# First MLP of a two-layer model: the v half before the u half, with LayerNorm and token mixing inside the groups of u

## The reference, cut to what matters

```python
def gmlp_mixer(h, w_in, b_in, ln_g, ln_b, w_s, b_s, w_out):
    B, S, _ = h.shape
    z = jax.nn.gelu(h @ w_in + b_in)
    u, v = jnp.split(z, 2, axis=-1)
    v = layer_norm(v, ln_g, ln_b)
    v = v.reshape(B, S // CHUNK, CHUNK, GMLP_GROUPS, GMLP_GROUP_DIM)
    causal = jnp.tril(jnp.ones((CHUNK, CHUNK), dtype=w_s.dtype))
    ws = w_s * causal[None]
    v = jnp.einsum('gts,bnsgc->bntgc', ws, v) + b_s.T[:, :, None]
    y = u * v.reshape(B, S, GMLP_WIDTH)
    return y @ w_out
```

## Time and profile before

| what | value |
|---|---|
| median of 3 runs | 2139.59 us (2136.43 to 2139.62) |
| the profiled execution, its own time | 2142.33 us |
| its span in the trace | 2140.6 us |
| mean granted TensorE clock | 0.971 of full speed |
| PE, share of the span | 93% |
| DVE, ACT, POOL | 39%, 33%, 48% |
| PE's share of the chain that ended last | 84% |
| first matmul of u, of v, of mlp_out | 52.9, 151.1, 264.3 us |

### The profile page before, as it was taken

One profiled execution on the slowest core, in us unless ns is written; L12 is line 12 of the kernel. 1 busy time (PEld: TensorE's weight loads), 2 busy tenths in 40 slices (PEclk: granted clock), 3 DMA queues, 4 the chain that ended last, 5 costly groups with the idle time before them and its releaser, 6 DMA issues.

```text
span 2140.6 us, 28567 instructions
## 1 busy us (share of the span) xinstructions
PE 1993.2 (93%) x10804; PEld 1703.4 (80%) x10804; DVE 836.9 (39%) x1442; ACT 714.4 (33%) x1112; POOL 1029.4 (48%) x553
## 2 busy tenths in 40 slices
PE   5999898999999979998998999999889998978997
PEld 5889887888888868876877888888767997856997
DVE  5545656534443066252635111100537730036212
ACT  3422334222221244444634222212433223335323
POOL 1644374466664435546634655544333343605552
PEclk9999999899999999999999999999999999998999
DMA  7645334465656213222112333322212325201132
GB/s 255 220 168 172 113 109 132 138 190 170 196 167 206 90 49 91 78 85 88 44 39 60 103 94 97 98 94 93 72 59 70 99 89 91 89 20 40 60 99 79
DMA packets 220321, 230.62 MB, mean 108 GB/s; under 512 B 15456, under 2 KB 185224, under 8 KB 219960
## 3 DMA queue, kind: packets, MB, share of 16 engines
q1 hardware_dynamic: 219712, 229.01, 34.8%
q10 hardware_dynamic: 504, 0.15, 0.0%
HBM read 226.33 MB, written 2.79 MB: 107 GB/s over the span
## 4 chain that ended last, share of the span: by engine, by line
PE 84%; DVE 6%; ACT 4%; issue 2%; POOL 1%; DMA 1%; ACTq 1%; DVEq 1%; SPq 0%; POOLq 0%
PE acc L1344 66%; PE aux L1344 4%; PE ms L625 3%; PE acc L600 2%; PE ms L1344 2%; PE ada_ps L1344 1%; PE aux L614 1%; PE ada_ps L1505 1%; DVE tmp L1946 1%; DMA x_tok<-in_x 1%; PE aux L1595 1%; PE aux L1632 1%; POOL w_lo L736 1%; DVE score L2160 1%; DVE ada_acc L1842 0%
## 5 line engine op out<-in xcount | busy, mean ns | idle before, releaser
L736 POOL TENSOR_TENSOR w_lo<-raw,w_hi 128x1024 fp32r<-128x1024 f32 (+1 forms) x296 | 742.4, 2522 | 639.8 <-ACT w_hi L729 639.4
L1344 PE MATMUL acc<-hh,w_hi 128*128 128x512 f32 (+1 forms) x1472 | 562.7, 382 | 45.8 <-issue 21.5
L1344 PE MATMUL acc<-hh,w_lo 128*128 128x512 f32 (+1 forms) x1472 | 555.1, 377 | 0.0
L1344 PE MATMUL acc<-hl,w_hi 128*128 128x512 f32 (+1 forms) x1472 | 554.9, 377 | 0.0
L729 ACT ACTIVATE w_hi<-raw 128x1024 fp32r<-128x1024 f32 (+1 forms) x296 | 308.4, 1051 | 409.6 <-DMA raw<-in_ffn_w_down 152.8
L1344 PEld LDWEIGHTS acc<-hh,w_hi 128*128 128x128 f32 x1472 | 285.2, 194 | 104.4 <-issue 48.6
L1344 PEld LDWEIGHTS acc<-hl,w_hi 128*128 128x128 f32 x1472 | 285.6, 194 | 49.3 <-issue 1.7
L1344 PEld LDWEIGHTS acc<-hh,w_lo 128*128 128x128 f32 x1472 | 285.0, 194 | 49.1
L1344 PE MATMUL acc<-w_hi,hh 128*128 128x256 f32 x704 | 201.1, 286 | 0.0
L1344 PE MATMUL acc<-w_hi,hl 128*128 128x256 f32 x704 | 199.2, 283 | 0.0
L1344 PE MATMUL acc<-w_lo,hh 128*128 128x256 f32 x704 | 199.2, 283 | 0.0
(11 more groups left out here) (472 smaller groups left out, 2972.8 us busy)
## 6 DMA issues: line engine op xcount, KB each, us to landing
raw<-in_ffn_w_gu SPq DMA_DIRECT2D x176, 256.0 KB, 3.2
ada_raw<-in_ada_w SPq DMA_DIRECT2D x80, 512.0 KB, 3.9
raw<-in_w_in SPq DMA_DIRECT2D x52, 512.0 KB, 3.4
raw<-in_ffn_w_down SPq DMA_DIRECT2D x44, 512.0 KB, 3.6
raw<-in_a_w_in SPq DMA_DIRECT2D x32, 512.0 KB, 4.8
raw<-in_a_w_out SPq DMA_DIRECT2D x16, 512.0 KB, 3.8
ada_raw<-in_kv_ada_w SPq DMA_DIRECT2D x16, 512.0 KB, 4.8
raw<-in_kv_w SPq DMA_DIRECT2D x16, 512.0 KB, 3.7
```

The source lines that it names most:

```text
L736: eng.tensor_tensor(w_lo[:, s, part, :], raw[:, s, part, :], w_hi[:, s, part, :].bitcast(F32), ALU.subtract).then_inc(w_split, 1)
L1344: ins = pe.matmul(out, w, x, start=first and n == 0, stop=last and n == len(pairs) - 1, skip_group_check=check)
```

## The change

v goes first, u second. The sixteen transposes go into group 1 of v, the row sums into groups 3 and 5, the spreading of the gain into group 7, each ahead of chunk 4 and with more PSUM banks. u follows; from its group 1 on, two mixings are put ahead of chunks 2 and 5 of each group. The last two mixings go ahead of chunks 2 and 3 of `mlp_out`. DVE handles a pair of mixings at the start of its work for a u group and the modulation slot after it. On ACT and POOL the rounding of a pair is part of the epilogue of a u group; the last pair and all weight units of `mlp_out` from unit 2 on come after it, in that order. In SP's list the slots 16 to 19 go behind units 2, 4, 6 of the first half and unit 0 of the second, and `ws_raw` is loaded into another place, two waits later. The first unit of `mlp_out` is computed with `apart`.

```diff
-            load_stage(sp, "mlp_u", lambda i, j: ada_slot_load(sp, 2 * i + j), skip=2, unroll=True)
-            load_stage(sp, "mlp_v", lambda i, j: ada_slot_load(sp, 8 + 2 * i + j), unroll=True)
+            load_stage(sp, "mlp_v", lambda i, j: ada_slot_load(sp, 2 * i + j), skip=2, unroll=True)
+            load_stage(sp, "mlp_u", lambda i, j: ada_slot_load(sp, 8 + 2 * i + j), unroll=True)
...
-            load_out("mlp_out", {(0, 7): 16, (1, 2): 17, (1, 3): 18, (1, 4): 19})
+            load_out("mlp_out", {(0, 2): 16, (0, 4): 17, (0, 6): 18, (1, 0): 19})
...
+            lead(act, "mlp_v", split_hi, epi_v, "mlp_u", unroll=True)
+            split_hi(act, S["mlp_u"], 0, 1)
             act.wait_ge(ln_moments, 1)
...
-            for x in range(GC // 2):
-                hi_chunks("y", 2, y_hi, 2 * x)
-                split_hi(act, S["mlp_out"], 0, 0, slice(x + 1, x + 2))
-            output_stage(0, "mlp_out", "gu0", "h1", xs_mlp, GC // 2)
+
+            def epi_u(st, i, j):
+                g = 2 * i + j
+                wait_sums(act, st, i, j)
+                for m in range(2):
+                    col = 2 * g + m
+                    ins = act.activation(u[:, col:col + 1, :], sums(j)[:, m:m + 1, :], ACT.Gelu_apprx_tanh, bias=par_b[:, 88 + col:89 + col])
+                ins.then_inc(acc_read["act"], 1)
+                if g:
+                    hi_chunks("y", 2, y_hi, 2 * (g - 1))
+            lead(act, "mlp_u", split_hi, epi_u, "mlp_out", unroll=True, started=True)
+            hi_chunks("y", 2, y_hi, GC - 2)
+            output_stage(0, "mlp_out", "gu0", "h1", xs_mlp, 2)
...
+            lead(pool, "mlp_v", split_lo, mask_weights, "mlp_u", unroll=True)
+
+            def low_tokens(st, i, j):
+                g = 2 * i + j
+                if g:
+                    lo_tokens(2 * g - 2)
+                    lo_tokens(2 * g - 1)
+            lead(pool, "mlp_u", split_lo, low_tokens, "mlp_out", unroll=True)
+            lo_tokens(GC - 2)
+            lo_tokens(GC - 1)
+            output_stage("mlp_out", "gu0", "h1", 2)
...
+            def token_weights(i, j, k):
+                if (i, j, k) == (0, 1, 4):
+                    pe.wait_ge(ws_masked, 1)
+                    for q in range(4):
+                        for n in range(4):
+                            ins = pe.transpose(WS_BANKS[q][:, n * P:(n + 1) * P], ws_raw[:, 4 * q + n, :], ident[:])
+                        ins.then_inc(wst_ps, 1)
+                if (i, j, k) == (1, 1, 4):
+                    pe.wait_ge(wst_ready, 4)
+                    for q in range(3):
+                        row_sums(q)
+                if (i, j, k) == (2, 1, 4):
+                    pe.wait_ge(r_read, 1)
+                    row_sums(3)
+                if (i, j, k) == (3, 1, 4):
                     pe.wait_ge(r_read, 4)
                     spread_gain(0)
-                wide_beside(8)(i, j, k)
...
+                wide_beside(0)(i, j, k)
+            gemm("mlp_v", hh, hl, h_ready, CH["h0"], unroll=True, before_chunk=token_weights)
...
+            def mixing_in_u(i, j, k):
+                g = 2 * i + j
+                if g and k in (2, 5):
+                    mix_tokens(2 * g - 2 + k // 5)
+                wide_beside(8)(i, j, k)
+            gemm("mlp_u", hh, hl, h_ready, CH["h0"], unroll=True, before_chunk=mixing_in_u)
+
             def mixing_beside(g, k):
-
-                if g == 0 and k + AHEAD < GC:
-                    mix_tokens(k + AHEAD)
+                if (g, k) in ((0, 2), (0, 3)):
+                    mix_tokens(GC - 4 + k)
                 if (g, k) == (0, 8):
                     wide_columns(3)
-            for g in range(AHEAD):
-                mix_tokens(g)
...
-                     mixing_beside, free=((mix_read, GC), (ada_col, ADA_SETUP - ADA_PAIRS + 4)))
+                     mixing_beside, free=((mix_read, GC), (ada_col, ADA_SETUP - ADA_PAIRS + 4)), apart=True)
...
+            def mixed_pair(p):
+                for g in (2 * p, 2 * p + 1):
                     c = CH["y"] + g
                     free_tmp(c)
                     dve.wait_ge(mix_ps, g + 1)
...
+                dve.wait_ge(acc_read["act"], S["mlp_u"].read0 + p + 3)
                 dve.drain()
...
+            def u_epilogue(st, i, j):
+                g = 2 * i + j
+                if g:
+                    mixed_pair(g - 1)
+                ada_slot(8 + g)
+            each_group("mlp_u", u_epilogue)
+            mixed_pair(GC // 2 - 1)
+            for slot in range(16, 20):
+                ada_slot(slot)
             first_products(0, y_mlp)
-            for slot in range(17, 20):
-                ada_slot(slot)
```

More of the change, by code:

```diff
@@ L98 @@
 STAGES = [
-    Stage("mlp_u", 4, DC, "act"), Stage("mlp_v", 4, DC, "dve", True), Stage("mlp_out", 1, GC, "dve", True, wide=True),
+    Stage("mlp_v", 4, DC, "dve", True), Stage("mlp_u", 4, DC, "act"), Stage("mlp_out", 1, GC, "dve", True, wide=True),
     Stage("gu0", 11, DC, "dve"), Stage("down0", 1, FC, "dve", True, wide=True),
@@ L210, in build_program @@
         x_first = place("x_first", [P, DC, T], at=ph + 16 * K)
-        ws_raw = place("ws_raw", [P, 16, P], at=ph + 48 * K)
+        ws_raw = place("ws_raw", [P, 16, P], at=ph)
         y_mlp = place("y_mlp", [P, NB, T], at=ph + 80 * K)
@@ L770, in _ @@
                 next_step(s)
-            load_group(sp, "mlp_u", 0, 0)
-            load_group(sp, "mlp_u", 0, 1)
+            load_group(sp, "mlp_v", 0, 0)
+            load_group(sp, "mlp_v", 0, 1)
             sp.wait_ge(ada_ready, ADA_SETUP - ADA_PAIRS)
-            sp.dma_start(ws_raw[:], io["a_w_s"][0].rearrange("g t s -> t g s")).then_inc(ws_in, 16)
             sp.dma_start(b_in[:], io["a_b_in"][0:1, GW:2 * GW].broadcast_to([P, GW])).then_inc(b_in_in, 16)
@@ L777, in _ @@
             sp.wait_ge(ada_first_ps, 1)
+            sp.dma_start(ws_raw[:], io["a_w_s"][0].rearrange("g t s -> t g s")).then_inc(ws_in, 16)
             sp.dma_start(q_bias[:].rearrange("p g t -> p (g t)"),
@@ L974, in _ @@
                 act.activation(x_first[:, k, :], XT_BANKS[k % len(XT_BANKS)], ACT.Copy).then_inc(kept_ready, 1)
-            split_hi(act, S["mlp_u"], 0, 0)
+            split_hi(act, S["mlp_v"], 0, 0)
             hi_chunks("h0", DC, hh)
[L978 to L985, removed]
             def epi_v(st, i, j):
@@ L1261, in nothing, with mask_weights @@
                 pass
-            split_lo(pool, S["mlp_u"], 0, 0)
+            split_lo(pool, S["mlp_v"], 0, 0)
             lo_chunks("h0", DC, hh, hl)
[L1265 to L1275, removed]
+            def mask_weights(st, i, j):
+                if (i, j) == (0, 0):
+                    pool.wait_ge(ws_in, 16)
+                    pool.affine_select(out=ws_raw[:], in_=ws_raw[:], compare_op=ALU.is_ge, fill=0.0, base=0,
+                                       pattern=[[0, 16], [-1, P]], channel_multiplier=1).then_inc(ws_masked, 1)
+            lead(pool, "mlp_v", split_lo, mask_weights, "mlp_u", unroll=True)
[8 more added lines that the diff above has]
+            output_stage("mlp_out", "gu0", "h1", 2)
             pool.nop().then_inc(act_ready, 2)
@@ L1561, in _, with row_sums @@
                 ada_column(s, s % 2)
[L1562 to L1579, removed]
+            WS_BANKS = [aux[:, 0, :], aux[:, 1, :], ms[:], ada_ps[:]]
+            R_BANKS = [aux[:, 0, :], aux[:, 1, :], ms[:], aux[:, 0, :]]
+            def row_sums(q):
+                pe.matmul(R_BANKS[q], ones[:], ws_t[:, 4 * q:4 * q + 4, :].rearrange("p g t -> p (g t)"), start=True, stop=True).then_inc(r_ps, 1)
+            def token_weights(i, j, k):
[13 more added lines that the diff above has]
+                if (i, j, k) == (3, 1, 4):
                     pe.wait_ge(r_read, 4)
                     spread_gain(0)
-                wide_beside(8)(i, j, k)
-            gemm("mlp_v", hh, hl, h_ready, CH["h0"], unroll=True, before_chunk=gain_and_columns)
-            pe.wait_ge(gain_ready, 1)
-            AHEAD = 4
+                wide_beside(0)(i, j, k)
+            gemm("mlp_v", hh, hl, h_ready, CH["h0"], unroll=True, before_chunk=token_weights)
             def mix_tokens(g):
@@ L1591, in mix_tokens @@
                     pe.wait_ge(v_norm_act, NB // 2 * (g // V_PART + 1))
+                if g == 0:
+                    pe.wait_ge(gain_ready, 1)
                 if g >= 2:
@@ L2001, in each_group, with weights_copies, token_bias @@
                     epilogue(st, g // 2, g % 2)
-            each_group("mlp_u", u_epilogue)
-            for q in range(4):
+            def weights_copies(q):
                 dve.wait_ge(wst_ps, q + 1)
[L2005 to L2009, removed]
+                dve.tensor_copy(ws_t[:, 4 * q:4 * q + 4, :].rearrange("p g t -> p (g t)"), (aux[:, 0, :], aux[:, 1, :], ms[:], ada_ps[:])[q]) \
+                    .then_inc(wst_ready, 1)
+            def token_bias(q):
                 dve.wait_ge(r_ps, q + 1)
+                src = (aux[:, 0, :], aux[:, 1, :], ms[:], aux[:, 0, :])[q]
```

(31 more changed lines are left out.)

6 lines of the change are left out of this document (removed).

## The result

The changed kernel takes 2155.97 us (median of 4 runs, 2151.81 to 2159.88), beside 2138.30 for the kernel before in the same session: a ratio of 1.0081, interval 1.0067 to 1.0096. It is slower by 17.7 us where 7.3 were forecast, and 1.0 us above the upper end of the range. The profiled execution, 2151.81, was the fastest of its four; its span of 2150.1 is only 9.5 longer than that of before, whose profiled execution lay 2.7 above its median.

What follows compares the result with a forecast made beforehand. PE, busy 93% of the span, was taken as the bound. Removed 12.5 us against added stalls: -12.5 + (4.6 + 2.5) + (6.2 + 2.5) + 4.0 = +7.3, so 2146.9 us, range 2136 to 2155.

Steps and rivals of the forecast that it cites:

- Removed, 12.5: PE waits at the hand-overs from v to the output product and from u to v vanish: 12.5 us saved.
- LayerNorm: Between v's end and the first mixing: 10.7 us lost before, afterwards covered by u's group 0.
- some 15: Sign that the forecast is right: first mixing some 15 us after v's end, no PE gap from v to u.
- The spatial weights: Transposes, row sums and mask, now inside v: 1.8 us lost before, 0 after; 0 to 2 if cover fails.
- A: Unit 2 of mlp_out, split after the last pair of y: PE idle 4.6 us, plus 2.5 for the clock.
- B: Unit 5 of mlp_out, its load behind slots 16 and 17: PE idle 6.2 us, plus 2.5 for the clock.
- C: Weights in u arrive late because their loads wait behind DVE's slot after the mixings: 4.0 us, bounds 0 and 12.
- R2: Rival, clearly slower: the u weights cost their upper bound of 12, +15.3 us, 2154.9; chance 0.12 including all above +11.
- The hand-over to gu0: End of mlp_out and gu0: waits hang on PE's own units as before, so no cost.
- a tail that changes by more than 1 us: Sign that the forecast is wrong: time after mlp_out longer or shorter than before by more than 1 us.
- R1: Rival, no change: DVE and POOL hardly meet in u, no cost there, +3.3 us, 2142.9; chance 0.30 with neighbours.
- R3: Rival, faster: mlp_out's unit 5 load not late and u costs nothing, -5.4 us, 2134.2; chance 0.12.

Runs made afterwards that it cites:

- e6: Changed kernel with e2, e3 and e4 together; 2123.55 us, ratio 0.9935 to the kernel before.
- e5: Changed kernel with e1, e3 and e4 together; 2126.77 us, ratio 0.9950 to the kernel before.
- e7: Changed kernel with u's two mixings per group ahead of chunks 1 and 3 instead of 2 and 5; 2141.80 us, ratio 1.0022 to the kernel before.
- e1: Changed kernel with DVE doing its modulation slot before the pair of mixings in u; 2143.26 us, ratio 1.0017 to the kernel before.
- e2: Changed kernel with SP's loads of modulation slots 8 to 15 one weight group later; 2143.86 us, ratio 1.0031 to the kernel before.
- e4: Changed kernel with modulation slots 16 to 19 back where the kernel before had them; 2144.74 us, ratio 1.0021 to the kernel before.
- e8: Changed kernel measured again, unedited; 2152.80 us, ratio 1.0070 to the kernel before.
- e3: Changed kernel with unit 2 of mlp_out split ahead of the last pair of y; 2145.78 us, ratio 1.0041 to the kernel before.

## Why the prediction came out as it did

**Removed, 12.5: right.** e6 has the change's order of work and none of its three stalls, and is 13.7 us faster than before. By the traces gu0's first matmul comes 13.8 us earlier in e6 (374.72 before, 360.88) and 13.0 in e5. LayerNorm is covered: the first mixing comes at 171.94, 15.4 us after DVE's last addition for v began (156.51), the "some 15" of the forecast. The spatial weights cost nothing inside v.

**A, 4.6 + 2.5: right.** The idle time is 4.51 or 4.52 in all six traces that have this stall. The clock took 1.5 us behind it in the first and 1.7 (e7), 2.5 (e1), 2.9 (e2), 3.1 (e4) and 3.1 (e8) in the others, 2.5 on average. e3 alone brings 7.6 us against e8 (15.5 - 7.9), A's forecast 7.1.

**B, 6.2 + 2.5: right in place, 7.2 + 1.6 in size in the first trace, 7.3 to 8.4 of idle and 2.0 to 3.1 of clock in the others.** The landing was 6.60, not the 5.5 chosen, so the idle time lay above the upper bound of 6.9. e4 alone brings 8.7 (15.5 - 6.8), the forecast 8.7.

**C, 4.0: the step that failed.** The prediction put it: "Half met, and landing 5.7 (between 4.8 and 6.2), the chain is 18.1, 1.3 too long ... of six such chains three pay: 4.0". The mechanism, the chain and its budget were right: chains of 20.6, 18.5 and 17.2 us against 16.8 were followed by gaps of 4.09, 2.00 and 0.45, and three did pay. The size was not. First, no clock was priced for C at all, though A and B had theirs; it fell after the gaps of 4.09 and 2.00 us and took 3.2 of the 5.7 us by which C was short in this trace (2.5 of idle time, 3.2 of clock). Second, the landing in the three chains was 6.4 to 7.0 where 5.7 was taken, above the row from which the upper end of 6.2 was read, and all these loads were issued two at a time right behind two slot loads; in e2, ahead of them, the median was 3.7. That added about a microsecond to each chain; the meetings, 3.0 us on average, were within the 3.5 taken for them. Third, one mean length stood for all: PE pays for the excess of the long chains and gets nothing back from the short. The bound of 20.7 was reached once, and it was none by the prediction's own terms, since it had every meeting but the landing at 4.8; with 6.2 it is 22.1. In all C cost 9.7 by the table by stretch, and by medians 10.2 (e1) or 9.6 (e2) against e8: near the upper bound of 12 that R2 used, not the 4.0 taken. In the other traces with this step unchanged it is 8.2 (e8), 9.7 (e3) and 12.6 us (e4), idle time and clock together.

**Sum.** The three stalls together were forecast at 7.1 + 8.7 + 4.0 = 19.8. From e8 to e6 they measure 2152.80 - 2123.55 = 29.3, and the single edits add up to 7.6 + 8.7 + 9.9 = 26.2. With the removed part, -13.74 + 29.25 = +15.51, the 15.5 found. Of the miss of 8.2 (15.5 less 7.3), C is some 6. By the trace of the changed kernel A is 6.0, B 8.8 and C 9.7, together 24.5; by that of e8 they are 25.6. That is the whole difference up to the last matmul of mlp_out, which starts at 380.05 and 381.13 in these two and at 355.58 in e6. The PE timeline shows what comes next, first e8, then e6:

```profile
387.52 0.55 PE L1350 MATMUL acc<-hh,w_hi 128*128 128x256 f32 x1 [5.99 <-issue]
```

```profile
360.88 0.55 PE L1352 MATMUL acc<-hh,w_hi 128*128 128x256 f32 x1 [4.91 <-issue]
```

The hand-over to gu0, put at no cost, takes 1.1 us more. The spans differ by 30.3 us, so 3.7 lie behind gu0's first matmul. In all ten traces the same work is done there, and it took from 1759.9 (e6) to 1766.5 us (e2), 1765.9 before; no run shows what sets it. At such a spread the prediction's sign of a tail that changes by more than 1 us can tell nothing: from mlp_out's last matmul on the changed kernel's first trace is 1.2 us shorter than that of before.

**The rivals.** R2 (2154.9) is what came out in time, though by its mechanism only in part: the meetings with POOL were not constant, and e1 shows that they cost PE nothing where the slot stands ahead of the mixings. The Trainium skill ("SBUF — State Buffer", the section "Who interferes with whom") has a DVE instruction with two SBUF inputs wait for the whole of the POOL instruction that holds the port. The rows at 178.7 agree: the first multiplication took 2.92 us beside a w_lo of 2.6 (half of the 5.21). But the rule tells nothing of how often they meet, and that was the open number. R1 (no cost in u) and R3 (no B) fell with the first reading of PE's gaps.

**What stays open.** Why the changed kernel's first median is 3.2 us above its second; and the spread from run to run. That C differs between executions is seen in four profiled ones (changed, e3, e4 and e8 have their gaps at different groups), so do the clock's losses and the part behind gu0, and the kernel with the least in its way, e6, has the least spread. How much of the spread each of them makes is not shown: e1, without gaps in u, still spreads over 8.4 us.

## What to carry to other kernels

When work of one engine moves, follow the queue that waits for that engine's side products: here a modulation slot, needed by nobody soon, stood in SP's list ahead of weights that PE needed at once, and its wait passed DVE's delay on to PE. A load should stand behind the wait of its own buffer alone, and a slot that is not urgent behind the weights. A chain near its budget is priced by its long cases and with the clock behind every gap, because the short cases give nothing back. And one trace is one execution: the same gap of 4.51 us was followed by a loss of 1.5 us in one and of 3.1 in another.

## What the runs showed of the hardware

The granted clock fell after PE idles of 2.00 us (changed kernel, 0.63 on average over the next 4.6 us) and of 1.80 us (e8, 0.66 over the next 5.1), but not after one of 2.10 us (e8). What was lost behind the same idle of 4.5 us differed from execution to execution, 1.5 to 3.1 us in six traces, and behind idles of 7.2 to 8.4 us it was 1.6 to 3.1. The 2.5 taken from the stall of 3.02 us in gu0 is the average of the first and close to that of the second (2.4).

In u and at the start of mlp_out, a 512 KB weight load landed in 3.7 us (median) where it was issued ahead of the modulation's loads (e2). Where two of them were issued right behind two of those, the median was 6.7 us in the changed kernel's first trace and 5.8 in e8, and single ones took 4.9 to 9.4.
